# Query and key projections of differential attention by seven quarter products, summed by GpSimd and VectorE

## The reference

```python
def diff_attention(x, w_qkv, w_o, lam, subln_g, lambda_init):
    q, k, v = jnp.split(x @ w_qkv, 3, axis=-1)      # x: 256 x 1024, w_qkv: 1024 x 3072
    q = q.reshape(B, S, DA_HEADS, 2, DA_HEAD_DIM)   # 8 heads of 2 x 64
    k = k.reshape(B, S, DA_HEADS, 2, DA_HEAD_DIM)
    v = v.reshape(B, S, DA_HEADS, 2 * DA_HEAD_DIM)
    ...
        s = jnp.einsum('bqhcd,bkhcd->bhcqk', q_blk, k).astype(jnp.float32) * scale
        s = jnp.where(causal, s, -jnp.inf)
        p = jax.nn.softmax(jnp.where(causal, s, -jnp.inf), axis=-1)
        attn = p[:, :, 0] - lam_full * p[:, :, 1]
        return jnp.einsum('bhqk,bkhe->bqhe', attn.astype(v.dtype), v)
    ...
    return o.reshape(B, S, D_MODEL).astype(x.dtype) @ w_o
```

## Time and profile before

| what | before |
|---|---|
| median of three runs | 1956.05 us (1954.45 to 1958.23) |
| the profiled execution | 1958.03 us, its span 1956.2 us |
| outside the span | 1.8 us |
| TensorE busy | 1647.6 us, 84% of the span, 12826 matmul records |
| VectorE, ScalarE, GpSimd busy | 35%, 19%, 10% |
| mean granted clock of TensorE | 0.93 of full speed (two levels, 1.2 and 2.4 GHz) |
| the chain that ended last | TensorE 59%, transfers 32%, VectorE 5%, ScalarE 2% |

### The profile page before, as it was taken

The page is one execution under the profiler, slowest core; times in us unless marked ns, Lnnn a source line. Parts: engine busy times, 40 slices in busy tenths (PEclk is TensorE's granted clock), DMA queues, the critical chain, the costliest instruction groups (busy, mean ns, idle before and its releaser), DMA issues.

```text
span 1956.2 us, 29793 instructions
## 1 busy us (share of the span) xinstructions
PE 1647.6 (84%) x12826; PEld 1038.9 (53%) x12826; DVE 679.4 (35%) x1163; ACT 370.8 (19%) x748; POOL 195.0 (10%) x91
## 2 busy tenths in 40 slices
PE   9999999999999998776666797999988778676664
PEld 7998986997995854222122242867954223221211
DVE  1564431464541265211111124573365211111103
ACT  1444101343211251000000011331211000000001
POOL 2331422331330000000000000000300000000000
PEclk9999999999999999978887998999999989987877
DMA  9341444251355438999999998222156999999994
GB/s 384 103 169 52 186 181 164 85 167 72 151 204 204 172 135 351 427 427 428 427 427 427 425 419 341 106 86 67 68 238 285 426 428 426 426 426 427 427 427 194
DMA packets 48228, 537.10 MB, mean 275 GB/s; under 512 B 4533, under 2 KB 12981, under 8 KB 15033
## 3 DMA queue, kind: packets, MB, share of 16 engines
q1 hardware_dynamic: 46752, 528.27, 65.9%
q10 hardware_dynamic: 1304, 6.51, 0.8%
HBM read 533.71 MB, written 1.05 MB: 273 GB/s over the span
## 4 chain that ended last, share of the span: by engine, by line
PE 59%; DMA 32%; DVE 5%; ACT 2%; issue 1%; POOL 0%; ACTq 0%; DVEq 0%
PE ps L450 48%; DMA extra<-in_moe_w_gu 12%; DMA arena<-in_moe_w_gu 9%; PE ps L462 8%; DMA arena<-in_moe_w_down 6%; DMA ring<-in_moe_w_gu 4%; PE ps L468 2%; DVE x L1545 1%; DVE arena L1534 1%; ACT arena L2459 1%; ACT arena L2455 1%; DVE arena L1539 1%; DVE arena L1545 0%; ACT L2455 0%; DMA tcom<-in_tcom 0%
## 5 line engine op out<-in xcount | busy, mean ns | idle before, releaser
L462 PE MATMUL ps<-arena 128*32 128x512 f32 (+1 forms) x1348 | 204.4, 689 | 81.3 <-DMA arena<-in_moe_w_gu 65.0
L450 PE MATMUL ps<-hT,ring 128*128 128x256 f32 (+1 forms) x1472 | 262.5, 336 | 0.0
L2459 ACT ACTIVATE arena<-ps 128x512 f32<-128x512 f32 (+4 forms) x150 | 90.2, 601 | 879.0 <-PE ps L462 493.3
L462 PE MATMUL ps<-ring,arena 128*32 128x512 f32 x1248 | 181.9, 715 | 88.5 <-DMA ring<-in_moe_w_gu 69.7
L450 PEld LDWEIGHTS ps<-hT,ring 128*128 128x128 f32 x1472 | 233.4, 191 | 25.6 <-issue 2.1
L1534 DVE TENSOR_TENSOR arena<-arena,ps 128x256 f32<-128x256 f32 (+3 forms) x119 | 64.5, 542 | 511.6 <-ACT arena L2455 433.7
L462 PEld LDWEIGHTS ps<-arena 128*32 128x32 f32 (+1 forms) x1348 | 48.9, 126 | 220.2 <-DMA arena<-in_moe_w_gu 97.5
L450 PE MATMUL ps<-arena 64*64 64x64 f32 (+11 forms) x1456 | 142.4, 344 | 26.3 <-ACT arena L2748 22.3
L450 PE MATMUL ps<-arena,ring 64*64 64x64 f32 (+3 forms) x1344 | 146.9, 292 | 3.1 <-ACT hT L2459 1.4
L462 PEld LDWEIGHTS ps<-ring,arena 128*32 128x32 f32 x1248 | 38.0, 121 | 207.0 <-DMA ring<-in_moe_w_gu 101.1
L450 PEld LDWEIGHTS ps<-arena,ring 64*64 64x64 f32 (+2 forms) x1344 | 129.1, 161 | 18.3 <-DVE arena L1545 1.8
(11 more groups left out here) (204 smaller groups left out, 1820.3 us busy)
## 6 DMA issues: line engine op xcount, KB each, us to landing
arena<-in_moe_w_gu SPq DMA_DIRECT2D x57, 2048.0 KB, 41.3
ring<-in_moe_w_gu SPq DMA_DIRECT2D x49, 2048.0 KB, 41.3
ring<-in_moe_w_down SPq DMA_DIRECT2D x35, 2048.0 KB, 41.3
arena<-in_moe_w_down SPq DMA_DIRECT2D x29, 2048.0 KB, 40.6
extra<-in_moe_w_gu SPq DMA_DIRECT2D x22, 2048.0 KB, 40.8
ring<-in_w_merge SPq DMA_DIRECT2D x16, 2048.0 KB, 8.2
ring<-in_w_in SPq DMA_DIRECT2D x9, 2048.0 KB, 7.3
ring<-in_attn_w_qkv SPq DMA_DIRECT2D x6, 2048.0 KB, 7.2
```

Source lines behind the costliest of these rows:

```text
L450: i = t.matmul(o, l, r, start=first, stop=last, skip_group_check=True)
L462: i = t.matmul(o, l, r, start=first, stop=last, skip_group_check=True)
L2459: s.activation(o, a, ACT.Copy).then_inc(*act.one(name))
```

## The change

Each chunk of q and k is seen as a 2 x 2 of quarters, in output columns and in contraction, and the input as a 2 x 2 of quarters, in contraction and in tokens. Seven products of such quarters give the four quarters of the result, with sums before and behind them:

- TensorE: `proj_qk` issues for each chunk the parts 1, 6, 7, 5 into one PSUM tile ("a") and 2, 4, 3 into another ("b"). A part is 8 matmuls of 128x128 moving tokens, 56 for a chunk. q0 and k0 go in one piece each; q1 and k1 are cut between the units at other places than before.
- GpSimd: `hsum` (four sums of 128x512 of the input, once, into the space of `mT`), and for each chunk four sums of 128x1024 of the weights: one written over a quarter of the chunk itself, s2, s1, and s4 which replaces s2 when part 6 has been multiplied. These go one chunk after the other as fast as their waits allow.
- ScalarE: `qk_out` copies one area of 128x256 (part 1) instead of 128x1024.
- VectorE: `first_sums` (four TENSOR_TENSOR of 128x256, each of an SBUF and a PSUM operand, after part 5) frees tile "a" by "half"; `last_sums` (three of them, after part 3) frees tile "b" by "out". `score` now waits for the "out" of VectorE. In the loop over units 0 to 3 one of first_sums(q1), last_sums(q1), first_sums(k1), last_sums(k1) follows each `back`.
- SyncE: a chunk of q or k frees its slot after part 3. The order of the transfers is the same.

The order on TensorE before, from the score of unit (0,1) to that of unit (1,0) (a line of dots stands for the other matmuls of the same piece). ps0 to ps3 are the PSUM tiles; the rows with ring1 are chunk q1, with ring2 chunk k1.

The diff, with the code that it moves:

```diff
--- before.py
+++ after.py
@@ -363,11 +363,16 @@
     d.oT = carve(2048).rearrange("p (k s) -> p k s", k=KT)
     d.o = carve(2048).rearrange("p (t n) -> p t n", t=NT)
     d.tmp, d.lneg, d.sub = carve(256), carve(1), carve(1)
+    assert at[0] <= OWN - 1024
     at[0] = OWN
     d.qT, d.kT = (carve(2048).rearrange("p (h s) -> p h s", h=8) for _ in range(2))
     d.v = carve(2048).rearrange("p (t n) -> p t n", t=NT)
     d.Sb, d.Pb, d.PTb = ([carve(512), carve(1024)] for _ in range(3))
     d.S2, d.P2 = ([carve(512), carve(1024)] for _ in range(2))
+    d.hsum = [flat(m.mT)[:, 512 * i:512 * i + 512].rearrange("p (k s) -> p k s", k=4) for i in range(4)]
+    d.s2 = [carve(1024).rearrange("p (k n) -> p k n", k=4) for _ in range(2)]
+    at[0] = OWN - 1024
+    d.s1 = carve(1024).rearrange("p (k n) -> p k n", k=4)
 
     at[0] = 0
     e = m.moe = Memory()
@@ -840,11 +845,33 @@
                 ps.held.discard(ps.of[n])
             return ps(n)
 
-        def proj_qk(name, half, *cs):
-            n = f"da {name}{half}"
-            p = opened(n, cs[0] == 0, cs[-1] == 3, (act, n))
-            mm(proj_T(wcols(m.w(n), KT, 512), hT, KT, [(p[:, c * 256:(c + 1) * 256], slice(c * P, (c + 1) * P)) for c in cs]),
-               n if cs[-1] == 3 else None)
+        def proj_qk(name, half, *parts):
+
+            n, c = f"da {name}{half}", ("q0", "k0", "q1", "k1").index(f"{name}{half}")
+            (a11, a12), (a21, a22) = quarters(wcols(m.w(n), KT, 512))
+            (b11, b12), (b21, b22) = [[hT[:, 4 * k:4 * k + 4, P * i:P * i + P] for i in range(NT)] for k in range(2)]
+            (h1, h2, h3, h4), s1, s2 = d.hsum, d.s1, d.s2[c % 2]
+            for q in parts:
+                late = q in (2, 4, 3)
+                name2 = n + (" b" if late else " a")
+                if q in (1, 2):
+                    tile(name2, *(((dve, n + " out"),) if late else ((act, n + " p1"), (dve, n + " half"))))
+                    ps.held.add(ps.of[name2])
+                if q in (5, 3):
+                    ps.held.discard(ps.of[name2])
+                p = ps(name2)
+                i, a, b = {1: (0, a11, b11), 6: (1, s2, h2), 7: (2, a21, h3), 5: (3, s1, h1), 2: (0, a12, b21), 4: (2, a22, h4), 3: (3, s2, b22)}[q]
+                if q == 1:
+                    t.wait_ge(*m.w.landed(n))
+                elif q == 6:
+                    t.wait_ge(*pool("da hsum"))
+                    t.wait_ge(*pool(n + " s2"))
+                elif q == 5:
+                    t.wait_ge(*pool(n + " s1"))
+                elif q == 3:
+                    t.wait_ge(*pool(n + " s4"))
+                mm([(p[:, 256 * i + P * e:256 * i + P * e + P], a[:, k, P * e:P * e + P], b[:, k, :], k == 0, k == 3)
+                    for e in range(2) for k in range(4)], f"{n} p{q}")
 
         def proj_v(half, i, ks=range(KT)):
             n = f"da v{half}"
@@ -858,8 +885,8 @@
         def score(g, i):
             SL, n = P * (i + 1), f"da{g}{i} score"
             p = tile(n, (dve, f"da{g}{i} sc"))
-            t.wait_ge(*act(f"da q{g // 2}"))
-            t.wait_ge(*act(f"da k{g // 2}"))
+            t.wait_ge(*dve(f"da q{g // 2} out"))
+            t.wait_ge(*dve(f"da k{g // 2} out"))
             mm([(p[:, cc * 512 + hl * SL:cc * 512 + (hl + 1) * SL], d.qT[64 * cc:64 * cc + 64, 2 * g + hl, i * P:(i + 1) * P],
                  d.kT[64 * cc:64 * cc + 64, 2 * g + hl, 0:SL], True, True) for hl in range(2) for cc in range(2)], n)
 
@@ -897,24 +924,24 @@
         final_norm(1)
         proj_v(0, 1)
         for name in "qk":
-            proj_qk(name, 0, *range(4))
+            proj_qk(name, 0, 1, 6, 7, 5, 2, 4, 3)
 
         score(*units[0])
-        proj_qk("q", 1, 0, 1)
+        proj_qk("q", 1, 1, 6, 7, 5)
         score(*units[1])
-        proj_qk("q", 1, 2, 3)
+        proj_qk("q", 1, 2, 4, 3)
         turned(*units[0])
         score(*units[2])
-        proj_qk("k", 1, 0)
+        proj_qk("k", 1, 1, 6)
         values(*units[0])
         turned(*units[1])
-        proj_qk("k", 1, 1)
+        proj_qk("k", 1, 7, 5)
         values(*units[1])
         score(*units[3])
-        proj_qk("k", 1, 2)
+        proj_qk("k", 1, 2, 4)
         turned(*units[2])
         proj_qk("k", 1, 3)
-        ps.late.add(ps.of["da k1"])
+        ps.late.add(ps.of["da k1 b"])
         values(*units[2])
         turned(*units[3])
         score(*units[4])
@@ -1926,6 +1953,29 @@
         ts(d.sub, vcol("subln"), 0.8, None, MUL, None, "da sub")
         units = [(g, i) for g in range(4) for i in (1, 0)]
 
+        def first_sums(name, half):
+
+            n = f"da {name}{half}"
+            p, dst = ps(n + " a"), (d.qT, d.kT)[name == "k"]
+            (c11, c12), (c21, c22) = [[dst[:, 4 * half + 2 * j:4 * half + 2 * j + 2, P * i:P * i + P] for i in range(NT)] for j in range(2)]
+            v.wait_ge(*act(n + " p1"))
+            tt(c12, c11, area(p, 1), ADD)
+            v.wait_ge(*pe(n + " p5"))
+            tt(c21, c12, area(p, 2), ADD)
+            tt(c22, c21, area(p, 3), ADD)
+            tt(c12, c12, area(p, 3), ADD, n + " half")
+
+        def last_sums(name, half):
+
+            n = f"da {name}{half}"
+            p, dst = ps(n + " b"), (d.qT, d.kT)[name == "k"]
+            (c11, c12), (c21, c22) = [[dst[:, 4 * half + 2 * j:4 * half + 2 * j + 2, P * i:P * i + P] for i in range(NT)] for j in range(2)]
+            v.wait_ge(*pe(n + " p2"))
+            tt(c11, c11, area(p, 0), ADD)
+            v.wait_ge(*pe(n + " p3"))
+            tt(c21, c21, area(p, 2), ADD)
+            tt(c12, c12, area(p, 3), ADD, n + " out")
+
         def front(g, i):
             n = f"da{g}{i}"
             if g > 1:
@@ -1965,9 +2015,13 @@
             ts(d.oT[:, 4 * half + 2:4 * half + 4, i * P:(i + 1) * P], ps(n)[:, 512:768].rearrange("p (k s) -> p k s", k=2), d.sub, None,
                MUL, None, n + " out b")
 
-        for n in range(4):
+        for name in "qk":
+            first_sums(name, 0)
+            last_sums(name, 0)
+        for n, more in enumerate((lambda: first_sums("q", 1), lambda: last_sums("q", 1), lambda: first_sums("k", 1), lambda: last_sums("k", 1))):
             front(*units[n])
             back(*units[n])
+            more()
         squares(1, 0)
         front(*units[4])
         normed(1, 0)
@@ -2651,8 +2705,8 @@
 
         def qk_out(name, dst, half):
             n = f"da {name}{half}"
-            s.wait_ge(*pe(n))
-            cp(dst[:, 4 * half:4 * half + 4, :], ps(n).rearrange("p (h s) -> p h s", h=4), n)
+            s.wait_ge(*pe(n + " p6"))
+            cp(dst[:, 4 * half:4 * half + 2, 0:P], area(ps(n + " a"), 0), n + " p1")
 
         def v_out(half):
             n = f"da v{half}"
@@ -2690,16 +2744,16 @@
         qk_out("q", d.qT, 0)
         qk_out("k", d.kT, 0)
         front(*units[0])
+        qk_out("q", d.qT, 1)
         front(*units[1])
-        qk_out("q", d.qT, 1)
         turned(*units[0])
         front(*units[2])
         values(*units[0])
         turned(*units[1])
+        qk_out("k", d.kT, 1)
         values(*units[1])
         front(*units[3])
         turned(*units[2])
-        qk_out("k", d.kT, 1)
         values(*units[2])
         turned(*units[3])
         rms(1, 0)
@@ -3004,6 +3058,32 @@
             both(s1, a11, s2, ADD, name + " s1")
             g.wait_ge(*pe(name + " p6"))
             both(s2, a12, s2, SUB, name + " s4")
+    d = m.diff
+    (b11, b12), (b21, b22) = [[m.hT[:, 4 * k:4 * k + 4, P * i:P * i + P] for i in range(NT)] for k in range(2)]
+    (h1, h2, h3, h4), s1 = d.hsum, d.s1
+    for c, name in enumerate(("q0", "k0", "q1", "k1")):
+        n, s2 = "da " + name, d.s2[c % 2]
+        (a11, a12), (a21, a22) = quarters(wcols(m.w(n), KT, 512))
+        g.wait_ge(*m.w.landed(n))
+        both(a21, a11, a21, SUB)
+        if c == 0:
+            g.wait_ge(*dve("l1 merged1"))
+            g.wait_ge(*pe("l1 d pv"))
+        both(s2, a22, a21, SUB, n + " s2")
+        if c:
+            g.wait_ge(*pe("da " + ("q0", "k0", "q1")[c - 1] + " p5"))
+        both(s1, a11, s2, ADD, n + " s1")
+        if c == 0:
+            g.wait_ge(*pe("l1 out1"))
+            for i in range(NT):
+                g.wait_ge(*act(f"fn{i} out a"))
+                g.wait_ge(*dve(f"fn{i} out b"))
+            both(h3, b22, b12, SUB)
+            both(h1, b12, b11, SUB)
+            both(h2, b22, h1, SUB)
+            both(h4, b21, h2, SUB, "da hsum")
+        g.wait_ge(*pe(n + " p6"))
+        both(s2, a12, s2, SUB, n + " s4")
     for l in range(2):
         M = f"moe{l} "
 
@@ -3126,7 +3206,7 @@
 
     wq = T["attn_w_qkv_2"][0]
     for name, c0 in (("v0", 2048), ("q0", 0), ("k0", 1024), ("q1", 512), ("k1", 1536), ("v1", 2560)):
-        cols("da " + name, wq, c0, 512, "da " + name)
+        cols("da " + name, wq, c0, 512, "da " + (name if name[0] == "v" else name + " p3"))
     for half in range(2):
         cols(f"da wo{half}", T["attn_w_o_2"][0], 512 * half, 512, "da out0")
```

## The result

The change is slower: 1961.49 us median of ten runs (1958.0 to 1965.43) against 1956.09 for the kernel before beside it, a ratio of 1.0029 with a 95% interval of 1.0019 to 1.0039. That is 5.4 us (3.7 to 7.6). The profiled execution takes 1964.64 us, its span 1962.8; TensorE is busy for 1636.7 us (1647.6 before), GpSimd for 238.9 us, 12% of the span (10%).

The account below looks back on a forecast made before the run. TensorE was taken to bound the attention stage, and the expert-weight stream from 790 us on. Waits ate 5.1 of 5.2 us gained (+0.1), the clock added 2.7: +2.8, median 1958.9 us; forecast's range 1957.9 to 1960.2, 8-in-10 range 1952.8 to 1962.4.

Parts of the forecast that it names:

- Products, q0 and k0: TensorE before the first score: seven quarter products per chunk, one every 1.79 us, saving 1.28 us a chunk; GpSimd keeps up.
- The three waits: TensorE waits 1.2 us before the values of (0,1), 1.4 before those of (0,0), 3.1 before score (1,0).
- The holding: VectorE operations in the attention units wait for GpSimd's sums: 0.1, 2.05 and 1.3 us lost.
- the 512 sum: VectorE's 128x512 sum in unit (0,1), held behind k1's first GpSimd sum, losing 2.05 us.
- the 128x4 operation: VectorE's TENSOR_SCALAR in the front of unit (0,0), held within GpSimd's last sum, losing 1.3 us.
- The 128x2 one: VectorE's TENSOR_SCALAR in the back of (0,1): not held in the forecast; held in a rival (+5.1 us, chance 0.20).
- The clock: TensorE's granted clock falls to half behind the wait before score (1,0), costing 2.7 us.
- The middle between two bounds: Clock loss behind the third wait taken as 2.7 us, between 2.2 (early fall) and 3.2 (fall at its end).
- The stage's sum: Attention stage: +0.1 us after waits eat 5.1 of 5.2 gained, plus 2.7 for the clock, +2.8 us.
- the first one: Opening step: whatever the attention stage gains or loses shifts everything behind it one for one, to the end.
- The rivals: Clock stays up: 1956.2, chance 0.20; VectorE and GpSimd miss each other: 1952.9, 0.10; one hold more: 1961.2, 0.20.
- the last one: Back of (0,1): 128x2 operation held, VectorE then waits a whole GpSimd sum (2.36 us); +5.1 us, 1961.2, chance 0.20.

Follow-up runs that it names:

- The tile's run: The change, with the tile of k1's first products left out of the turn when score (1,0) takes its tile; 1961.08 us, 1.0022 of the kernel before.
- the run with GpSimd reordered: The change, with k1's first two GpSimd sums before q1's last and k1's third after the back of (0,1); 1963.57 us, 1.0029 of the kernel before.
- the wait filled: The change, with 27 tiny 64x64x64 products added on TensorE between the values of (0,0) and score (1,0); 1959.66 us, 1.0008 of the kernel before.
- the three together: The change, with the tile out of the turn, GpSimd's last four sums in VectorE's waits, and 60 more idle TensorE instructions; 1952.95 us, 0.9973 of the kernel before.

## Why the prediction held, and where it failed

The measured 1961.49 lies within the range, 2.6 us above the forecast, and with 0.29% beyond the 0.2% that was to count as no change. The way to it was only half right, and that the time fell into the range is in part luck: the stage gave 2.3 us of the 5.4.

- **Products, q0 and k0**: right. They start every 1.79 us, a chunk takes 12.5, GpSimd keeps up, and the first score is 2.75 us earlier, for 2.7 in the working.
- **The three waits**: right in place and cause, 1.51, 1.37 and 2.79 us for 1.2, 1.4 and 3.1. The tile's run shows the third as a wait for the turn of the tiles.
- **The holding**: the 512 sum lost 2.04 us (2.05 in the working) and the 128x4 operation 1.05 (1.3). The 128x2 one was held too, which the forecast had left out: 0.5. The Trainium skill, "SBUF — State Buffer", "Who interferes with whom", had spoken for it, and the trace now agrees: 0.73 us for 0.23.
- **The clock**: it fell where the working put it, but cost 1.6 us and not 2.7. The middle between two bounds was too dear here; in the run with GpSimd reordered, behind a wait as long, the same stretch took 3.0 us more than with the wait filled (10.77 against 7.80).
- **The stage's sum**: +2.3 for +2.8.
- **The step that failed** is the first one: "what the attention stage gains or loses shifts everything behind it one for one, to the end". It named the work that would move and not the program itself. 394 more instructions ahead of the experts put their code elsewhere against the 16 KB packets. In the two profiles of the change that cost 2.8 us at the gaps and behind them, more than all of the stage, and it goes when 60 or 108 instructions more are added. Another 0.8 of the longer expert stretch lies where the weights stream, and its cause stays open. The page of the profile has a line for the packets' queue, and the sum had no term for it.
- **The rivals**: the last one gave 1961.2, 0.3 from the median, by accident. Its small operation was held, but VectorE's 1024 sum came 0.08 us ahead of GpSimd's, so the whole sum of 2.36 was not waited for; the time came from the experts.

Not settled: which few instructions decide (behind the 48 records 404 cost 13.5 us, 394 from 1.8 to 3.8, and 198, 256, 454 and 502 nothing), and the recurrent layer, which took 282.4 to 286.9 us over all runs, with both of the kernel before in the lower half and no order by place.

## What to carry to other kernels

Count the instructions that a change adds to an engine as a term of its own, and read a stretch that the change doesn't touch in both traces: where the same records there take longer with no semaphore between them, move the code by some idle instructions before judging the idea. Sums of GpSimd belong into the windows where VectorE waits for exponentials, and a tile whose readers are late belongs out of the turn: the three together made 4.5 us faster than before what was 5.4 us slower.

## What was not expected of the hardware

Instructions that do no useful work, put ahead of code that doesn't change, moved that code's time by 13 us or by nothing, by their number alone (404 or 256). And a lead of 0.08 us was enough to settle who of VectorE and GpSimd goes first: the later one waited until the other's operation had ended, GpSimd's sum (3.35 us for 2.36) as well as VectorE's TENSOR_SCALAR of 128x2 (0.73 for 0.23).
